# Further tiles of a mixture-of-experts layer: places for three weights of their own, loads and gathers ahead, counts in registers

## The reference

```
def moe_ffn(h, w_router, router_bias, w_gate, w_up, w_down):
    ...                                   # each token picks 2 of 16 experts, all in one group of 4
    out = jnp.zeros_like(h)
    for e in range(N_EXPERTS):            # 16
        y = (jax.nn.silu(h @ w_gate[e]) * (h @ w_up[e])) @ w_down[e]
        out = out + gates[:, e:e + 1].astype(h.dtype) * y
    return out
```

## Time and profile before

| | us |
|---|---|
| three runs, median | 2750.52 |
| lowest and highest of them | 2746.09, 2758.64 |
| the profiled execution | 2748.48 |
| its span, first to last instruction | 2746.7 |
| mean granted TensorE clock | 0.931 of full speed |

### The profile page before, as it was taken

How to read it: one execution, slowest core, us unless ns; L and a number is a source line. 1 busy time by engine, 2 the same in 40 slices (tenths; PEclk the granted TensorE clock), 3 DMA queues, 4 the chain that set the end, 5 groups by cost and what they waited for, 6 DMA issues and landing times. The chain is left out here.

```text
span 2746.7 us, 29276 instructions
## 1 busy us (share of the span) xinstructions
PE 2376.1 (87%) x11414; PEld 1894.0 (69%) x11414; DVE 1626.9 (59%) x2311; ACT 1333.4 (49%) x2010; POOL 122.1 (4%) x118
## 2 busy tenths in 40 slices
PE   8999889999999889999899856999949866999952
PEld 6887668888887767788666635777737654777721
DVE  5556346555556345555535475988865576888802
ACT  5555345555555435555234313777722433787700
POOL 0001000000001000000000000000021000000001
PEclk9999889999999889999999977999969987999976
DMA  7664545665665344666234526999943026999842
GB/s 259 234 225 148 210 179 169 230 215 208 221 219 193 124 154 169 238 230 230 77 105 159 181 81 225 374 378 380 370 163 123 17 85 214 381 388 380 328 184 86
DMA packets 174381, 585.94 MB, mean 213 GB/s; under 512 B 14832, under 2 KB 23472, under 8 KB 141968
## 3 DMA queue, kind: packets, MB, share of 16 engines
q1 hardware_dynamic: 151968, 501.85, 51.1%
q10 hardware_dynamic: 15632, 57.87, 5.3%
q0 software_dynamic: 6624, 24.12, 2.4%
HBM read 536.52 MB, written 47.28 MB: 213 GB/s over the span
## 5 line engine op out<-in xcount | busy, mean ns | idle before, releaser
L315 DVE TENSOR_TENSOR LO<-RAW,HI 128x1024 fp32r<-128x1024 f32 x558 | 659.8, 1221 | 220.7 <-ACT HI L301 219.3
L301 ACT ACTIVATE HI<-RAW 128x1024 fp32r<-128x1024 f32 x558 | 569.0, 1053 | 393.2 <-PE PS L373 192.2
L371 PE MATMUL PS<-HI,FR 128*128 128x512 f32 (+2 forms) x1808 | 698.6, 386 | 29.4 <-DVE LO L315 8.7
L373 PE MATMUL PS<-HI,FR 128*128 128x512 f32 (+2 forms) x1808 | 691.6, 383 | 0.0
L372 PE MATMUL PS<-LO,FR 128*128 128x512 f32 (+2 forms) x1808 | 691.0, 382 | 0.0
L301 ACT ACTIVATE HI<-RAW,SM 128x512 fp32r<-128x512 f32 (+2 forms) x576 | 360.4, 681 | 309.0 <-PE PS L373 159.4
L317 DVE SCALAR_TENSOR_TENSOR LO<-RAW,SM,HI 128x512 fp32r<-128x512 f32 (+2 forms) x576 | 378.9, 709 | 210.6 <-ACT HI L301 210.3
L371 PEld LDWEIGHTS PS<-HI,FR 128*128 128x128 f32 x1808 | 345.0, 191 | 101.1 <-DVE LO L315 11.3
L373 PEld LDWEIGHTS PS<-HI,FR 128*128 128x128 f32 x1808 | 344.7, 191 | 66.2
L372 PEld LDWEIGHTS PS<-LO,FR 128*128 128x128 f32 x1808 | 344.9, 191 | 62.8
L439 DVE TENSOR_TENSOR FR<-PS,FR 128x512 fp32r<-128x512 f32 x224 | 144.3, 676 | 171.9 <-ACT FR L435 171.8
(11 more groups left out here) (292 smaller groups left out, 2327.8 us busy)
## 6 DMA issues: line engine op xcount, KB each, us to landing
RAW<-in_w_ffn_in SPq DMA_DIRECT2D x88, 1024.0 KB, 5.1
RAW<-in_w_gate SPq DMA_DIRECT2D x68, 1024.0 KB, 7.9
RAW<-in_w_up SPq DMA_DIRECT2D x68, 1024.0 KB, 7.3
RAW<-in_w_down SPq DMA_DIRECT2D x68, 1024.0 KB, 8.2
RAW<-in_w_ada SPq DMA_DIRECT2D x48, 1024.0 KB, 4.8
RAW<-in_w_ffn_out SPq DMA_DIRECT2D x44, 1024.0 KB, 4.9
RAW<-in_w_in SPq DMA_DIRECT2D x44, 1024.0 KB, 5.0
YD<-CN ACTq DMA_DIRECT2D x24, 1024.0 KB, 4.9
```

The costliest lines, as they stand in the source:

```text
L301: e.activation(HI[:, i % NSPLIT, c], raw_of(j)[:, c], ACT.Copy, scale=1.0 if g is None else g).then_inc(*hi_done.up())
L315: e.tensor_tensor(LO[:, i % NSPLIT, c], raw_of(j)[:, c], hi, ALU.subtract).then_inc(*lo_done.up())
L371: e.matmul(o, h, hi[:, j, :], start=first and k + j == 0, stop=False)
L373: x = e.matmul(o, ll, hi[:, j, :], start=False, stop=end)
```

## The change

Only the further tiles and what stands right behind them change.

- The semaphore `more_w` becomes three: `more_gate`, `more_up`, `more_down`. Gate and up stay in `RAW`, but begin one slot behind the last chunk of the first tiles, so gate can be loaded when the chunk two before the last is split (`lo_done.at(last_part(n - 2))`). Down gets four places of 512 KB in `SC` and is four DMAs instead of two. It waits for the last store of the first tiles and for the routing's `slots`.
- The waits for `y in` at the end of the bodies on PE, DVE and POOL, and SP's for `y`, are gone. In their place each user waits for the same piece's last user one expert back (`more_before`: expert k-1, whether it had a tile or not): SP's gate for `ab 0`, up for `ab 1`, down for `y`; POOL's gather for `xT`; PE's last product for ACT's `y in`.
- POOL's first gather of a further tile waits for the transposes of expert 14 instead of for the end of the first tiles.
- SP and ACT load all 16 counts into registers once, behind their first wait, and compare against these; PE, DVE and POOL still load each count in front of its branch.
- Behind the walk, PE waits for all of ACT's further work, and SP waits for its own loads and for all of PE's (`more_pe` at `m{l} all`), in both layers, whether a further tile ran or not.

```
-        def where_over(e, q, k, limit, mine, body):
+        def more_raw(l, i):
+            return RAW[:, (parts[edge[l] - 1][0] + 1 + i) % NRAW, :]
+        more_w = [SC[:, 0:1024], SC[:, 1024:2048], x_y1, x_fold_t]
+        def more_before(l, j, k):
+            return f"m{l} more {j} {k - 1}" if k else f"m{l} more {j - 1} {NE - 1}" if j > 1 else None
+        def where_over(e, q, k, limit, mine, body, counted=None):
-            value = e.value_load(CNT[0:1, k:k + 1], min_val=0, max_val=512)
+            value = load_count(e, k) if counted is None else counted[k]
...
             def body():
+                held = counted
                 if j == 1:
                     first()
+                    if early:
+                        held = [load_count(e, k) for k in range(NE)]
...
# pe_further
-                q.wait_ge(*more_w.at(f"{s} w up"))
-                for v in range(2):
+                for v, landed in enumerate((more_gate, more_up)):
+                    q.wait_ge(*landed.at(f"{s} w"))
...
-                q.wait_ge(*more_w.at(f"{s} w down"))
+                q.wait_ge(*more_down.at(f"{s} w"))
+                if more_before(l, j, k):
+                    q.wait_ge(*more_act.at(f"{more_before(l, j, k)} y in"))
...
-                q.wait_ge(*more_act.at(f"{s} y in"))
...
+            more_pe.also(f"m{l} all")
+            q.wait_ge(*more_act.at(f"m{l} all"))
# act_further
-            further(e, q, l, 1, [more_act, more_yd], first, one)
+            further(e, q, l, 1, [more_act, more_yd], first, one, True)
+            more_act.also(f"m{l} all")
# dve_further
-                q.wait_ge(*more_act.at(f"{s} y in"))
# pool_further
-                q.wait_ge(*pe.at(f"m{l} done"))
+                q.wait_ge(*pe.at(f"m{l} xT 141"))
...
+                if more_before(l, j, k):
+                    q.wait_ge(*more_pe.at(f"{more_before(l, j, k)} xT"))
...
-                q.wait_ge(*more_act.at(f"{s} y in"))
# sp_further
-                q.wait_ge(*lo_done.at(edge[l] - 1))
+                q.wait_ge(*lo_done.at(last_part(n - 2)))
...
+                prev = more_before(l, j, k)
+                for v, (w, landed) in enumerate((("w_gate_2", more_gate), ("w_up_2", more_up))):
+                    if prev:
+                        q.wait_ge(*more_pe.at(f"{prev} ab {v}"))
+                    if v:
+                        q.wait_ge(*lo_done.at(last_part(n)))
...
+                q.wait_ge(*dve.at(f"m{l} slots"))
+                q.wait_ge(*yd_out[1].at(f"m{l} y 15"))
+                if prev:
+                    q.wait_ge(*more_pe.at(f"{prev} y"))
+                for i in range(4):
+                    e.dma_start(more_w[i], A["w_down_2"][l, k].rearrange("(p k) c -> p k c", p=P)[:, i, :]).then_inc(
+                        *more_down.up(by=16))
...
-            further(e, q, l, 1, [more_w], first, one)
+            further(e, q, l, 1, [more_gate, more_up, more_down], first, one, True)
+            for landed in (more_gate, more_up, more_down):
+                q.wait_ge(*landed.last())
+            q.wait_ge(*more_pe.at(f"m{l} all"))
```

More of the change, by code:

```diff
@@ L162, in build @@
             "x_landed", "mod_stored", "gain_landed", "hd_stored", "yd_stored", "xg_landed", "yg_landed"))
-        more_pe, more_act, more_dve, more_w, more_xg, more_yd = (count(f"more_{n}") for n in (
-            "pe_done", "act_done", "dve_done", "weight_landed", "xg_landed", "yd_stored"))
+        more_pe, more_act, more_dve, more_gate, more_up, more_down, more_xg, more_yd = (count(f"more_{n}") for n in (
+            "pe_done", "act_done", "dve_done", "gate_landed", "up_landed", "down_landed", "xg_landed", "yd_stored"))
         C, at = {}, 0
@@ L1873, in where_over, with load_count, further @@
             q.met = met
-        def further(e, q, l, j, mine, first, one):
+        def load_count(e, k):
+            return e.value_load(CNT[0:1, k:k + 1], min_val=0, max_val=512)
+        def further(e, q, l, j, mine, first, one, early=False, counted=None):
             def body():
+                held = counted
                 if j == 1:
                     first()
+                    if early:
+                        held = [load_count(e, k) for k in range(NE)]
                 for k in range(NE):
-                    where_over(e, q, k, P * j, mine, lambda: one(k, j, f"m{l} more {j} {k}"))
+                    where_over(e, q, k, P * j, mine, lambda: one(k, j, f"m{l} more {j} {k}"), held)
                 if j + 1 < X_TILES[l]:
-                    further(e, q, l, j + 1, mine, first, one)
+                    further(e, q, l, j + 1, mine, first, one, early, held)
             where_over(e, q, NE, P * j, mine, body)
@@ L1898, in one @@
                 q.wait_ge(*more_dve.at(f"{s} xT in"))
[L1899 to L1900 removed]
+                for v, landed in enumerate((more_gate, more_up)):
+                    q.wait_ge(*landed.at(f"{s} w"))
                     for i in range(8):
                         x = e.matmul(PS[2 + v][:, :], x_g[1][:, P * i:P * i + P],
[L1903 removed]
+                                     more_raw(l, 2 * v + i // 4)[:, 512 * (i % 4):512 * (i % 4) + 512], start=i == 0, stop=i == 7)
                     x.then_inc(*more_pe.up(f"{s} ab {v}"))
@@ L1977, in sp_further @@
         def sp_further(e, q, l):
+            n = parts[edge[l] - 1][0]
             def first():
-                q.wait_ge(*lo_done.at(edge[l] - 1))
+                q.wait_ge(*lo_done.at(last_part(n - 2)))
             def one(k, j, s):
-                for v, w in enumerate(("w_gate_2", "w_up_2")):
+                prev = more_before(l, j, k)
[4 more added lines that the diff above has]
+                        q.wait_ge(*lo_done.at(last_part(n)))
@@ L1983, in one @@
                     for i in range(2):
-                        e.dma_start(RAW[:, 2 * v + i, :].rearrange("p (k c) -> p k c", k=4),
+                        e.dma_start(more_raw(l, 2 * v + i).rearrange("p (k c) -> p k c", k=4),
                                     A[w][l, k].rearrange("(p k) c -> p k c", p=P)[:, 4 * i:4 * i + 4, :]).then_inc(
-                                        *more_w.up(by=16))
-                more_w.also(f"{s} w up")
-                q.wait_ge(*more_pe.at(f"{s} ab 0"))
@@ L1989, in one @@
-                for i in range(2):
-                    e.dma_start(RAW[:, i, :].rearrange("p (k c) -> p k c", k=2),
-                                A["w_down_2"][l, k].rearrange("(p k) c -> p k c", p=P)[:, 2 * i:2 * i + 2, :]).then_inc(
-                                    *more_w.up(by=16))
-                more_w.also(f"{s} w down")
-                q.wait_ge(*more_pe.at(f"{s} y"))
+                                        *landed.up(by=16))
+                    landed.also(f"{s} w")
+                q.wait_ge(*dve.at(f"m{l} slots"))
@@ L1996, in sp_further @@
+                q.wait_ge(*yd_out[1].at(f"m{l} y 15"))
[4 more added lines that the diff above has]
+                        *more_down.up(by=16))
+                more_down.also(f"{s} w")
             q.wait_ge(*dve.at(f"m{l} counts"))
-            further(e, q, l, 1, [more_w], first, one)
+            further(e, q, l, 1, [more_gate, more_up, more_down], first, one, True)
```

5 lines of the change are left out of this document (2 added, 3 removed).

## The result

The changed kernel took 2733.09 us in the median of 10 runs (2728.71 to 2740.26); the kernel before 2749.3 in 10 runs beside it (2744.85 to 2758.64). The ratio is 0.9938 with an interval of 0.9924 to 0.9953: 17 us, or 0.6%, faster. The forecast was 2731.5 with a range of 2719 to 2741. The profiled execution has a span of 2730.5 (before: 2746.7).

A forecast was written before the change was run, and what follows sets the result against it. A serial chain around the two layer 1 further tiles, with engines mostly waiting, was taken as the bound. 8.1 + 3.2 + 10.6 - 3.0 = 18.9 off 2748.48 gives 2729.6; runs' median 2.0 above; forecast 2731.5, range 2719 to 2741.

The forecast's parts named there:

- What bounds the kernel: From last first-tile copy to YD gathers: a serial chain of gathers, two tiles and count walks, engines mostly waiting.
- Start of the first further tile: PE's first further product with gate begins at 2619.4 instead of 2627.53, 8.1 us earlier.
- PE's own chain: First further tile: banks free, count load and branch, then transposes to product; 2618.0, or 2619.5 with the gather's delay.
- The 1.5 for the half megabyte: Early first gather adds 0.52 MB to the full DMA stream, delaying the first tiles' end 1.5 us (bounds 0 and 1.5).
- The forecast's 2611.6 for the gate load: SP issues the first further gate at 2611.6, after 16 count loads taking 8.3 us; 2609.08 before.
- Between the tiles: PE idles 10.8 us between the two further tiles instead of 13.97, 3.2 earlier (bounds 2.0 and 7.5).
- The first rival: Between the tiles: lookahead works across the skipped expert, 8.6 us more won, 2723 in all; chance 0.05.
- Inside the tiles: Inside the second tile nothing changes; each tile could be up to 1.7 us faster or slower; counted 0.
- The tail: Second store to first YD gather takes 8.5 us instead of 19.1, 10.6 earlier, ACT's skips costing 0.4 each.
- the slower rival: ACT's walk without loads stalls on branch fetches; at 6.3 us a jump 71 longer, about 2802; chance 0.04.
- The border: Layer 0's end: held wqkv_b loads run beside the YD gathers, 3.0 us later (bounds 0 and 5.6).
- the dearer collision of its rival: Border costs its bound 5.6 and PE's step 1.2 more: 2735 to 2736; chance 0.21, shared with several terms short.

The follow-up runs named there:

- changed again: The changed kernel itself, measured and profiled a second time beside later runs: 2736.14 us, ratio 0.9946 to the kernel before.
- act_loads: Changed kernel, but ACT loads each expert's count ahead of its branch, as the kernel before did: 2742.09 us, ratio 0.9961.
- two_back: Changed kernel, but every wait for a further tile's predecessor names the expert two back instead of one back: ratio 0.9899.
- over_one_again: Second measurement of over_one, unchanged: 2719.9 us, ratio 0.9883 to the kernel before.
- over_one_p15: over_one, but POOL's first further gather waits for DVE's product of expert 15 instead of the transposes of expert 14: ratio 0.9876.
- late_gather: Changed kernel, but POOL's first further gather waits for PE's last first-tile product, as before: ratio 0.9987.
- over_one: Changed kernel; loads and gathers wait two experts back, one back only where it has a tile; SP's border waits in the taken branch: 2717.21 us, 0.9880.
- before_border: Kernel before, plus only SP's wait behind its walk for all of PE's further work, in both layers: ratio 1.0031.

## Why the prediction came out

**What bounds the kernel.** The chain was read rightly: every stage that was named moved the way that was named, and no other moved by more than unchanged code does, save where the clock differed. The size of the border and of the tiles came out otherwise.

**Start of the first further tile.** 8.1 earlier was forecast, and -10.3 + 2.2 = 8.1 was measured, with errors inside. The transposes had the right bound, PE's own chain. SP's 16 loads cost 0.6 each, 9.9 and not 8.3; the prediction named that price and its loss (1.3). Here the loss was covered, because PE's last product was itself late by the low clock; in the four kernels where it was less late (changed again, act_loads, two_back, over_one_again: 3.9 to 4.7) it cost 0.4 to 1.2 us, and in over_one_p15, at full clock, 3.5. The 1.5 for the half megabyte doesn't show (65.0 against 65.3 us, see late_gather); the clock took its place with some 2 us. That this stage came out at its forecast is luck. The forecast's 2611.6 for the gate load was wrong by the unchanged code's shift as well: read from the store of expert 15, gate was forecast 3.6 ahead and stands 4.9 ahead of it, right behind the 16 loads, so the loads are what holds gate, as said.

**Between the tiles.** 3.2 forecast, 2.1 measured, and the reason was right: both loads stood behind PE's Else side of the skipped expert. The term was mis-sized by the gather's landing, 11.4 and not 9.7, with gate, up and now down queued beside it; PE's step took 0.4 and not 1.1. The first rival (a lookahead that works, 8.6 more) was priced too low: two_back and over_one, in which the lookahead does work, have 10.8 and 10.9 less idle time than the changed kernel.

**Inside the tiles.** 0 with 1.7 either way for each; 2.7 was won in the first in one profile and 0.2 lost in the other. The shorter pause (1.6 instead of 11.1) doesn't settle it. From the product with gate to the end of the last product the first tile took 27.9 and 28.0 behind the long pause in the kernels before and before_border, but 26.0 behind as long a one in late_gather; behind the short one it took 25.0 to 25.1 in seven profiles, 23.4 and 26.0 in one each, and 28.1 and 28.0 in the changed kernel's second profile and in two_back. The last product is 7.13 at a granted clock of 1.00 throughout and 8.83 where the clock falls for part of it. The changed kernel's second profile, and its window 2650 to 2652 inside that product:

```profile
2648.93 8.83 PE L1932 MATMUL PS<-SC 128*128 128x512 f32 x16 [0.78 <-DVE SC L1977]
```

```profile
2650.00:2652.00 2.00, 2.00 (x3) 0.68 (x2) 0.00 (x0) 0.00 (x0) 0.00 (x0) 0.50 0.00 0
```

So the term that the sum had at 0 was mis-sized, and so was its bound of 1.7: in the mean of these profiles the tile gains behind a short pause (25.6 against 27.3), but by how much in one execution is the clock's, and no row of the kernel before could tell it.

**The tail.** 10.6 forecast, 9.8 measured. ACT's step was 0.36 (0.4 forecast); the store took 4.1 to land and not 2.6. No stall: the slower rival falls with the row of twelve branches at 45 ns. The Trainium skill, Runtime: NRT & Kernel Launch, section Instruction fetch mechanics, lets only a jump out of the fetched window stall; the trace agrees, since ACT's short jumps take 45 ns for the branch, and PE's jump over all further code 3.87 us in the changed kernel and 6.30 before. The rival looked for the stall in the wrong place: ACT's one long jump, in layer 0, is where it grew.

**The border.** 3.0 forecast, 6.4 measured, 5.9 by before_border alone: over the bound of 5.6 that the prediction set, so the dearer collision of its rival is what happened. The step that failed is what the loads collide with. It counted only the gathers of `YD`, which had an idle queue before; these lost 2.3, and 2.9 in before_border, near the forecast's 3.0. The other 4.1 (3.0 in before_border) is lost ahead of the first gather, on two things that the prediction left out. The last `YD` store lands late when it goes out behind the loads: 5.8 to 8.2 in the five kernels where it did, and 3.5 in before_border, where it went out 0.9 ahead of them. And ACT's jump to its Else side takes 5.2 to 6.2 beside the loads instead of 2.5 to 2.8. The later of the two releases POOL: the store in the changed kernel and late_gather (by 0.7 and 0.4), ACT's jump in the other four (changed again, before_border, act_loads, two_back). Either alone would hold the gather for most of the time, so the store's landing and the jump don't add up.

The prediction also took PE's event from the earlier trace rows, 2000.5, as fixed. PE's sequencer comes to its branch 4 to 5 us ahead of the last store, while the last products still run, and the event is the end of the jump that begins there. With SP's loads in flight that jump takes 6.1 to 7.7 us over the kernels; with SP held it takes 3.5 to 4.8, so the held loads go out from 1.6 ahead of the store to 0.9 behind it, at the very moment at which the end of the experts needs the queues.

The Trainium skill, DMA: Bandwidth & Descriptors, section Queues, rings and completion order, has queues share an engine by turns; by halves, an estimate by that rule, the store would have gone from 2.9 to 5.8. It took 5.8, 6.0, 6.5, 7.2 and 8.2 behind the loads: that rule's figure is the least of what was measured.

**The sum.** The terms that missed by more than a microsecond: border +3.4, the tile's products -2.7 (in this profile), between the tiles +1.1, and within the first term three that cancelled. That the sum came out at 17 to the forecast's 19 is partly their cancelling, and so luck. In the changed kernel's second profile the same short stages add up to 12.6 us won, not 16.3. Luck too is that ACT's first add stands at 2012.70 beside the forecast's 2013: 4.0 of unchanged code and 3.4 of the border cancel.

## What to carry to other kernels

A wait behind a skipped branch runs in every execution: ask at what moment its event comes, and what else needs the DMA queues then, a store, a gather, or a long jump's instruction fetch. A lookahead by one item of a list with holes looks at a hole; name the item whose buffer is really in use, in a branch of its own if need be. Counts held in registers pay on the engine whose walk is the path (7 us on ACT) and cost on one whose first transfer stands behind all the loads (up to 3.5 us on SP).

## What wasn't expected of the hardware

- The far jump over code that isn't run depends on the DMA traffic: ACT's took 2.5 to 2.8 us with SP's four loads mostly in and 5.2 to 6.2 with them just issued, PE's 3.5 to 4.8 with SP held and 6.1 to 7.7 with its loads in flight.
- A 512 KB store that landed after 2.9 in layer 0 and 2.6 at the end of the kernel before took 8.2 behind four 1 MB loads, and 10.9 beside gate, up and down; an indirect gather of the same size took 5.1, 7.1, 9.7 and 11.4, by what was queued beside it. The last two, in the changed kernel behind the first tile:

```profile
YD<-SC ACTq DMA_DIRECT2D x1, 512.0 KB, 10.9
SC<-HD,IDX POOLq DMA_INDIRECT x1, 11.4
```

- Behind the same pause of 3.4 us the granted clock fell to 0.50 for part of one product in some profiles and not in others, by different amounts for the same program, which moved the path by 1.4 to 2.9 us (8.1 to 8.2 against 9.6 to 11.0 from store to store), as much as a term of the sum.
- Loading 16 counts into registers took 9.9 us on SP (0.27 for the load, 0.6 with what belongs to it), longer than a gate piece of 1 MB takes to land (6.2).
